# An expert stage's Silu and gate product for the next step, placed ahead of the result copies on ScalarE and VectorE

## The chip, the cores and the metric

The kernel runs on one core of one Trainium2 chip. The metric is the device time of one execution in microseconds (us); lower is better. Times are given as the median of several runs.

## What is computed

The reference is one layer of a streaming encoder: a modulated RMSNorm, an attention of two head groups, an output projection, and then a mixture of 32 experts of which each token takes two. The change is in the experts alone. What they compute, cut to the core:

```python
def expert_step(acc, args):
    wg, wu, wd, cw = args
    hh = jax.nn.silu(x @ wg) * (x @ wu)
    return acc + (hh * cw[:, None].astype(hh.dtype)) @ wd, None
```

There are 1088 tokens (1024 of the prompt and 64 of the sample), the model's width is 1024 and an expert's is 256. All is in float32.

## The kernel before, in words

The program goes through its stages one after the other: modulation and projection, attention, the output projection with the router, the experts (`experts`), and the final sum and norm (`finish`). The router writes lists that say which tokens go to which expert, in blocks of 64 rows.

The experts run in steps. A step p handles two blocks side by side, one in partitions 0 to 63 and one in 64 to 127, with the weights of two experts: those of the first half (`a_gu`, `a_dn`) stay in three slots and are loaded by SyncE when a slot is free, those of the second half (`b_gu`, three buffers, and `b_dn`, two) are loaded anew for each step by ScalarE's queue. Gate and up weights of an expert are 2 MB, the down weights 1 MB. In these runs there are 26 steps, numbered 0 to 25; the program counts them two to a round, and the rounds beyond a sure minimum stand under a branch.

What one step does, and on which engine:

- GpSimd reads the list (`listing`, L1545), gathers the 128 token rows by an indirect DMA (`gather`, L1550), and at the end scatters the 128 result rows of 4 KB to `expert_rows` in DRAM by an indirect DMA (L1572).
- TensorE transposes the rows (`transpose_x`, L1584), multiplies by gate and up (`gate_up`, L1595 and L1598, 32 matmuls into one of two PSUM banks `gu_ps`), transposes the hidden rows (`transpose_hidden`, L1605), and multiplies by the down weights (`down`, L1618 and L1621, 16 matmuls into the single `y_ps`).
- ScalarE and VectorE each move half of the transposed rows from PSUM (`move_xT`, L1671 and L1737). ScalarE computes Silu of the gate half (`silu`, L1677), VectorE multiplies by the up half (`gate_times_up`, L1741) and copies the transposed hidden rows (L1749). Both copy half of the result from `y_ps` to the single tile `y`, with the router's weight as scale: the *result copies*, L1695 on ScalarE and L1754 on VectorE.

The order is written out by hand, one body for each engine, and semaphores tie the bodies together. TensorE's body for step p is: `gate_up(p + 1)`, `transpose_hidden(p)`, `transpose_x(p + 2)`, `down(p)`. These are the waits that matter around the change:

- A result copy of step p waits for `down(p)` and for the landing of the scatter of step p - 1, since both use the one tile `y`. The scatter of step p waits for both result copies.
- `down(p + 1)` waits for the result copies of step p, since there is one `y_ps`.
- `silu(p + 1)` waits for `gate_up(p + 1)` and for `transpose_hidden(p)`, since there is one tile `gate`. `gate_times_up(p + 1)` waits for `silu(p + 1)`, and `transpose_hidden(p + 1)` for that.
- ScalarE issues the load of `b_dn` for step p + 2 behind its result copy, and the load of `b_gu` for step p + 3 at the head of its body. SyncE's load of an `a` slot (L1503 and L1505 on SPq) waits for a `down` (`y_ready`).

Of the kernel before, what the change touches and what calls it, by code (L numbers as in the profile page):

```python
# [1441 lines left out]
def experts(nc, s, a, k):  # L1442
# [33 lines left out]
    def look(eng, first, n, low, high):  # L1476
        return eng.value_load(table[0:1, first + n:first + n + 1], min_val=low, max_val=high)
# [13 lines left out]
    def following(eng, p, n, do):  # L1491

        if p // 2 < SURE:
            do()
        elif p < STEPS:
            with eng.If(n > p // 2):
                do()
            with eng.Else():
                eng.nop()

    def weights(eng, ex, gu, dn, gu_sem, dn_sem):
        if gu is not None:
            eng.dma_start(gu, a["w_gu"][bass.ds(ex, 1)].rearrange("a p k n -> p (a k) n")).then_inc(gu_sem, 16)  # L1503
        if dn is not None:
            eng.dma_start(dn, a["w_dn"][bass.ds(ex, 1)].rearrange("a p k n -> p (a k) n")).then_inc(dn_sem, 16)  # L1505

    @block.sync
    def _(sp):
        def load(m):
            r = m % SLOTS  # L1510
            ex = look(sp, T_HELD, m, 0, NE - 1) if m else look(sp, T_FIRST, 0, 0, NE - 1)
            weights(sp, ex, a_gu[:, r, :, :], a_dn[:, r, :, :], slot_ld[r], slot_ld[r])

        def landed(m):
            sp.wait_ge(slot_ld[m % SLOTS], 32 * (m // SLOTS + 1))
            sp.sem_inc(loaded, 1)

        def where(m, body):
            with sp.If(loads > m):
                body(m)  # L1520
            with sp.Else():
                sp.nop()

        def follow(m):
            last = look(sp, T_FREE, m - SLOTS, 1, STEPS)
            alone(sp, y_ready, last, waited)
            load(m)

        load(0)
        sp.wait_ge(table_set, 1)  # L1530
        loads = look(sp, T_LOADS, 0, 1, NE)
        landed(0)
        sp.wait_ge(gu_ld[1], 16)
        where(1, load)
        sp.wait_ge(dn_ld[1], 16)
        where(2, load)
        for m in range(NE - 1):
            where(m + 1, landed)
            if m + SLOTS < NE:
                where(m + SLOTS, follow)  # L1540
# [117 lines left out]
    @block.scalar  # L1658
    def _(act):
        def expert(p):  # L1660
            return look(act, T_EXPERT, p, 0, NE - 1)

        def load_gu(p, ex):
            weights(act, ex, b_gu[p % 3][:, :, :], None, gu_ld[p % 3], None)

        def load_dn(p, ex):
            weights(act, ex, None, b_dn[p % 2][:, :, :], None, dn_ld[p % 2])

        def move_xT(p):
            act.wait_ge(xT_ready, p + 1)  # L1670
            act.activation(xT[:, 0:4, :], xT_ps[:, 0:4, :], ACT.Copy).then_inc(xT_out_act, 1)  # L1671

        def silu(p):
            act.wait_ge(gu_ready, p + 1)
            if p:
                act.wait_ge(hT_ready, p)
            act.activation(gate[:, :], gu_ps[p % 2][:, 0:DE], ACT.Silu).then_inc(gate_done, 1)  # L1677

        held = [expert(p) for p in range(3)]
        for p in range(2):  # L1680
            load_gu(p, held[p])
            load_dn(p, held[p])
        move_xT(0)
        n = look(act, T_ROUNDS, 0, 1, ROUNDS)
        following(act, 2, n, lambda: load_gu(2, held[2]))
        silu(0)
        move_xT(1)

        def body(p, n):
            following(act, p + 3, n, lambda: load_gu(p + 3, expert(p + 3)))  # L1690
            following(act, p + 2, n, lambda: move_xT(p + 2))
            act.wait_ge(y_ready, p + 1)
            if p:
                act.wait_ge(scattered, 16 * p)
            act.activation(y[:, 0:512], y_ps[:, 0:512], ACT.Copy, scale=entry[:, p, 2:3].bitcast(F32))\  # L1695
               .then_inc(y_out_act, 1)
            following(act, p + 2, n, lambda: load_dn(p + 2, expert(p + 2)))
            if p % 2 == 0:
                silu(p + 1)
            else:  # L1700
                following(act, p + 1, n, lambda: silu(p + 1))

        in_rounds(act, n, body)

    @block.vector
    def _(dve):
        own = Own(dve, own_dve)
        blocks = nb[:, :, :].rearrange("p a n -> p (a n)")
        one = consts[:, K_ONES:K_ONES + 2 * NE]
        own(dve.tensor_scalar(some[:, :], blocks, 0.0, None, ALU.is_gt))  # L1710
        own(dve.tensor_tensor(first[:, :], ended[:, :], blocks, ALU.subtract), wait=False)
        own(dve.tensor_tensor_scan(rank[:, :], one, some[:, :], 0.0, ALU.mult, ALU.add))
        own(dve.scalar_tensor_tensor(first[:, :], first[:, :], steps[:, 0:1], some[:, :], ALU.is_lt, ALU.mult))
        own(dve.tensor_reduce(cols[:, 4:5], first[:, :], AX.X, ALU.add), wait=False)
        own(dve.tensor_tensor(held[:, :], done[:, 0, :], some[:, :], ALU.mult))
        own(dve.tensor_reduce(count[:, :], held[:, :], AX.X, ALU.add))
        own(dve.scalar_tensor_tensor(cols[:, 1:2], count[:, :], 1.0, cols[:, 4:5], ALU.add, ALU.min))
        own(dve.tensor_scalar(count[:, :], cols[:, 1:2], -1.0, None, ALU.add))
        own(dve.tensor_scalar(ahead_i[:, :], count[:, :], 86.0, None, ALU.mult))
        own(dve.tensor_scalar(ahead_i[:, :], ahead_i[:, :], 8, None, ALU.logical_shift_right))  # L1720
        own(dve.tensor_copy(over[:, :], ahead_i[:, :]))
        own(dve.scalar_tensor_tensor(cols[:, 0:1], over[:, :], -float(SLOTS), count[:, :], ALU.mult, ALU.add))
        own(dve.tensor_scalar(held[:, :], rank[:, :], index, None, ALU.is_le))
        own(dve.tensor_reduce(count[:, :], held[:, :], AX.X, ALU.add))
        own(dve.tensor_scalar(over[:, :], count[:, :], float(NE), -float(NE), ALU.is_ge, ALU.mult))
        own(dve.tensor_tensor(count[:, :], count[:, :], over[:, :], ALU.add))
        own(dve.tensor_scalar(cols[:, 2:3], count[:, :], float(NE - 1), None, ALU.min))
        own(dve.tensor_scalar(held[:, :], rank[:, :], -1.0, index, ALU.add, ALU.is_le))
        own(dve.tensor_tensor(held[:, :], held[:, :], blocks, ALU.mult))
        own(dve.tensor_reduce(count[:, :], held[:, :], AX.X, ALU.add))  # L1730
        dve.tensor_tensor(cols[:, 3:4], count[:, :], steps[:, :], ALU.min).then_inc(cols_done, 1)
        dve.wait_ge(table_ready, 1)
        dve.tensor_copy(table[:, T_SLOT:T_ROUNDS], y_ps[0:1, 0:4 * LOOK + 1]).then_inc(table_set, 1)

        def move_xT(p):
            dve.wait_ge(xT_ready, p + 1)
            dve.tensor_copy(xT[:, 4:8, :], xT_ps[:, 4:8, :]).then_inc(xT_out_dve, 1)  # L1737

        def gate_times_up(p):
            dve.wait_ge(gate_done, p + 1)  # L1740
            dve.tensor_tensor(gate[:, :], gate[:, :], gu_ps[p % 2][:, DE:2 * DE], ALU.mult).then_inc(hidden_done, 1)  # L1741

        move_xT(0)
        gate_times_up(0)
        move_xT(1)

        def body(p, n):
            dve.wait_ge(hT_ready, p + 1)
            dve.tensor_copy(hT[:, :, :], hT_ps[:, 0:2 * P].rearrange("p (c n) -> p c n", c=2)).then_inc(hT_out, 1)  # L1749
            following(dve, p + 2, n, lambda: move_xT(p + 2))  # L1750
            dve.wait_ge(y_ready, p + 1)
            if p:
                dve.wait_ge(scattered, 16 * p)
            dve.tensor_scalar(y[:, 512:1024], y_ps[:, 512:1024], entry[:, p, 2:3].bitcast(F32), None, ALU.mult)\  # L1754
               .then_inc(y_out_dve, 1)
            if p % 2 == 0:
                gate_times_up(p + 1)
            else:
                following(dve, p + 1, n, lambda: gate_times_up(p + 1))

        in_rounds(dve, look(dve, T_ROUNDS, 0, 1, ROUNDS), body)


# [175 lines left out]
```

## Time and profile before

| What | Value |
|---|---|
| Median of 3 runs | 1358.05 us (1355.63 to 1359.54) |
| The profiled execution's own time | 1351.79 us |
| Its span | 1349.6 us |
| TensorE busy over the span | 1161.5 us (86%) |
| VectorE, ScalarE, GpSimd busy | 518.6, 342.2, 295.1 us |
| DMA moved | 218.56 MB, mean 162 GB/s |

The page puts the program's work beside each other by engine: busy time over the whole span, then the span in 40 slices, then the queues, the chain that ended last, and the costliest groups. In the slices the experts' stage is the stretch from about 923 to 1294 us. Both TensorE and the DMA engines are busy for 8 or more tenths of most of its slices. The page's chain that ended last covers only the last few per cent of the span, so the stage has to be read from its waits and its timeline.

### The profile page before, as it was taken

The page shows a single profiled execution, that of the slowest core. Times are in us where ns is not written, and L with a number is a line of the kernel's source. Part 1 is how long each engine was busy: PE and PEld are TensorE (multiplying, and loading weights), DVE is VectorE, ACT ScalarE, POOL GpSimd, SP SyncE. Part 2 cuts the span into 40 slices and gives each one's busy share as a digit, 9 for nine tenths or more (in the row PEclk, how much of TensorE's full clock was granted, in tenths as well). Part 3 has the DMA queues.
Part 4 walks back from the last instruction along what each step waited for, and adds up shares of the span by engine and source line. Part 5 has one row for each costly group of instructions (what it writes and reads, how often), then busy time and mean ns, then how long its engine had stood idle before and what let it go on. Part 6 is the DMA issues. An engine that isn't in the chain of part 4 may idle for free. (4 is left out here: it accounts for less than half of the span.)

```text
span 1349.6 us, 19893 instructions
## 1 busy us (share of the span) xinstructions
PE 1161.5 (86%) x7175; PEld 767.0 (57%) x7175; DVE 518.6 (38%) x1320; ACT 342.2 (25%) x854; POOL 295.1 (22%) x233
## 2 busy tenths in 40 slices
PE   4688999999999999999886999951998999899846
PEld 2346888888888888888773555521333333333312
DVE  2432244444444444535533466653112121111118
ACT  4422233333332333333442222110101011111102
POOL 2031313030302121110002565533112221211001
PEclk9677999999999999999998999975999899999978
DMA  9771202020102121110130111115998999999646
GB/s 372 291 287 50 71 19 89 1 88 3 60 11 70 53 78 45 54 53 26 47 140 8 63 53 57 47 32 236 419 393 313 386 379 388 376 374 363 249 185 250
DMA packets 53538, 218.56 MB, mean 162 GB/s; under 512 B 9904, under 2 KB 26680, under 8 KB 42560
## 3 DMA queue, kind: packets, MB, share of 16 engines
q1 hardware_dynamic: 36912, 117.26, 23.7%
q10 hardware_dynamic: 7632, 82.05, 15.3%
q0 software_dynamic: 8896, 17.93, 3.4%
q8 instruction: 63, 1.03, 0.3%
q14 instruction: 35, 0.29, 0.1%
HBM read 196.62 MB, written 30.03 MB: 168 GB/s over the span
## 5 line engine op out<-in xcount | busy, mean ns | idle before, releaser
L729 PE MATMUL att_piece_ps<-hT_hi,w_hi 128*128 128x384 f32 (+1 forms) x528 | 185.2, 351 | 2.0 <-DVE att_k_lo_sb L857 0.8
L1595 PE MATMUL moe_gu_ps<-moe_a_gu_sb,moe_xT_sb 128*64 x416 | 184.4, 596 | 2.0 <-DVE moe_xT_sb L1737 2.0
L1598 PE MATMUL moe_gu_ps<-moe_b_gu_sb,moe_xT_sb 128*64 128x512 f32 x416 | 184.4, 596 | 0.0
L729 PE MATMUL att_piece_ps<-hT_hi,w_lo 128*128 128x384 f32 (+1 forms) x528 | 173.6, 329 | 0.0
L729 PE MATMUL att_piece_ps<-hT_lo,w_hi 128*128 128x384 f32 (+1 forms) x528 | 173.2, 328 | 0.0
L916 DVE COPY att_pT_sb<-att_pT_ps 128x512 f32<-128x512 f32 (+2 forms) x192 | 94.6, 521 | 134.0 <-PE att_pT_ps L790 133.4
L1200 PE MATMUL mix_y_ps<-mix_w_out_sb,mix_oT_sb 128*128 128x512 f32 (+1 forms) x288 | 127.2, 600 | 2.2 <-ACT mix_oT_sb L1268 2.2
L1595 PEld LDWEIGHTS moe_gu_ps<-moe_a_gu_sb,moe_xT_sb 128*64 128x64 f32 x416 | 57.2, 138 | 121.2 <-issue 121.2
L977 ACT ACTIVATE att_probs_sb<-att_probs_sb,att_nmax_sb 128x640 f32<-128x640 f32 (+5 forms) x144 | 101.2, 703 | 42.1 <-DVE att_nmax_sb L902 41.3
L902 DVE CUSTOM_DVE_ANT_0 att_probs_sb<-att_s_ps,att_bias_sb 128x640 f32<-128x640 f32 (+5 forms) x144 | 95.2, 662 | 26.8 <-PE att_s_ps L778 14.6
L729 PEld LDWEIGHTS att_piece_ps<-hT_hi,w_hi 128*128 128x128 f32 x528 | 99.8, 189 | 9.4 <-issue 4.7
L992 ACT ACTIVATE keep_rows_all_sb<-att_o_ps,att_rden_sb 128x64 f32<-128x64 f32 x144 | 37.2, 309 | 261.0 <-PE att_o_ps L811 261.0
L706 POOL CAST w_hi<-att_w_raw_sb 128x1024 fp32r<-128x1024 f32 x21 | 21.8, 1038 | 364.8 <-PE att_piece_ps L729 331.7
L1618 PE MATMUL moe_y_ps<-moe_a_dn_sb,moe_hT_sb 128*64 x208 | 99.2, 621 | 1.5 <-DVE moe_hT_sb L1749 0.7
L729 PEld LDWEIGHTS att_piece_ps<-hT_lo,w_hi 128*128 128x128 f32 x528 | 100.0, 189 | 0.0
L729 PEld LDWEIGHTS att_piece_ps<-hT_hi,w_lo 128*128 128x128 f32 x528 | 99.7, 189 | 0.0
L1621 PE MATMUL moe_y_ps<-moe_b_dn_sb,moe_hT_sb 128*64 128x512 f32 x208 | 99.2, 621 | 0.0
L1754 DVE TENSOR_SCALAR moe_y_sb<-moe_y_ps,moe_entries_sb 128x512 f32<-128x512 f32 x26 | 19.5, 751 | 204.2 <-DMA expert_rows<-moe_y_sb,moe_entries_sb 193.5
L1200 PEld LDWEIGHTS mix_y_ps<-mix_w_out_sb,mix_oT_sb 128*128 128x128 f32 (+1 forms) x288 | 52.9, 186 | 69.9 <-issue 67.0
L790 PE MATMUL att_pT_ps<-keep_consts_sb,att_probs_sb 128*128 128x128 f32 (+2 forms) x560 | 87.6, 278 | 1.8 <-ACT att_probs_sb L977 1.7
L1572 POOL DMA_INDIRECT expert_rows<-moe_y_sb,moe_entries_sb x26 | 26.2, 1010 | 254.0 <-DVE moe_y_sb L1754 254.0
L805 PE MATMUL att_o_ps<-att_pT_sb,att_v_rows_sb 128*64 128x128 f32 (+1 forms) x1088 | 74.4, 277 | 7.7 <-DVE att_pT_sb L916 6.5
(280 smaller groups left out, 1801.6 us busy)
## 6 DMA issues: line engine op xcount, KB each, us to landing
moe_b_gu_sb<-in_w_gu ACTq DMA_DIRECT2D x26, 2048.0 KB
moe_b_dn_sb<-in_w_dn ACTq DMA_DIRECT2D x26, 1024.0 KB
moe_a_gu_sb<-in_w_gu SPq DMA_DIRECT2D x10, 2048.0 KB
keep_rows_all_sb<-in_w_ada SPq DMA_DIRECT2D x8, 2048.0 KB, 12.2
att_w_raw_sb<-in_w_qkv SPq DMA_DIRECT2D x21, 512.0 KB, 3.3
moe_a_dn_sb<-in_w_dn SPq DMA_DIRECT2D x10, 1024.0 KB
in_w_ada_sb<-in_w_ada SPq DMA_DIRECT2D x4, 2048.0 KB, 11.5
in_x_sb<-in_x_prompt SPq DMA_DIRECT2D x8, 512.0 KB, 7.0
```

What stands on the lines that cost most here:

```text
L729: ins = pe.matmul(bank[:, 0:hi - lo], w[:, kind, kc, :], x[:, kc, lo:hi], start=(m == 0), stop=(m == 3 * NC - 1))
L790: ins = pe.transpose(pT_ps[e % 2][0:m, b - b0, 0:r], probs[h][0:r, b * P:b * P + m], ident[0:r, 0:r])
L805: ins = pe.matmul(o_ps[head, 0:r], v, pT[h][0:m, b, 0:r], start=(b == 0), stop=(b == len(kb) - 1))
L902: dve.tensor_tensor_reduce(probs[h][0:r, 0:wide], s_ps[h][0:r, 0:wide], bias, -SCALE, BIG, ALU.add, ALU.min, nmax[0:r, 2 * at + h:2 * at + ...
L916: ins = dve.tensor_copy(pT[h][:, b0:b1, :], pT_ps[e % 2][:, 0:b1 - b0, :])
L977: act.activation(probs[h][0:r, 0:wide], probs[h][0:r, 0:wide], ACT.Exp, bias=nmax[0:r, 2 * at + h:2 * at + h + 1], scale=-1.0, accum_out=d ...
L992: ins = act.activation(rows_all[0:r, t, first + HD * h:first + HD * h + HD], o_ps[0:r, P + HD * h:P + HD * h + HD], ACT.Copy, scale=rden[0 ...
L1200: ins = pe.matmul(y_ps[0:r, 512 * n:512 * n + 512], oT[:, c, 0:r], w_out[:, c, 512 * n:512 * n + 512], start=(c == 0), stop=(c == NC - 1))
L1595: pe.matmul(gu_ps[p % 2][LANE[0], :], xT[:, c, LANE[0]], a_gu[:, bass.ds(slot, 1), c, :].rearrange("p a n -> p (a n)"), start=(c == 0), st ...
L1598: ins = pe.matmul(gu_ps[p % 2][LANE[1], :], xT[:, c, LANE[1]], b_gu[p % 3][:, c, :], start=(c == 0), stop=(c == NC - 1))
L1618: pe.matmul(y_ps[LANE[0], half], hT[:, c, LANE[0]], a_dn[:, bass.ds(slot, 1), c, half].rearrange("p a n -> p (a n)"), start=(c == 0), stop ...
L1621: ins = pe.matmul(y_ps[LANE[1], half], hT[:, c, LANE[1]], b_dn[p % 2][:, c, half], start=(c == 0), stop=(c == 1))
```

## The change

In the body of step p, ScalarE now does `silu(p + 1)` before `move_xT(p + 2)`, where it did it as the last thing, behind the result copy of step p and the issue of the `b_dn` load. VectorE now does `gate_times_up(p + 1)` behind `move_xT(p + 2)` and before its result copy, where it did it behind the copy. TensorE's, GpSimd's and SyncE's programs are the same. No instruction is added or removed but some branches.

```diff
@@ ScalarE's body
             following(act, p + 3, n, lambda: load_gu(p + 3, expert(p + 3)))
+            if p % 2 == 0:
+                silu(p + 1)
+            else:
+                following(act, p + 1, n, lambda: silu(p + 1))
             following(act, p + 2, n, lambda: move_xT(p + 2))
             act.wait_ge(y_ready, p + 1)
...
             following(act, p + 2, n, lambda: load_dn(p + 2, expert(p + 2)))
-            if p % 2 == 0:
-                silu(p + 1)
-            else:
-                following(act, p + 1, n, lambda: silu(p + 1))
@@ VectorE's body
             following(dve, p + 2, n, lambda: move_xT(p + 2))
+            if p % 2 == 0:
+                gate_times_up(p + 1)
+            else:
+                following(dve, p + 1, n, lambda: gate_times_up(p + 1))
             dve.wait_ge(y_ready, p + 1)
...
                .then_inc(y_out_dve, 1)
-            if p % 2 == 0:
-                gate_times_up(p + 1)
-            else:
-                following(dve, p + 1, n, lambda: gate_times_up(p + 1))
```

VectorE's order in the first steps of the experts, before. L1749 copies the transposed hidden rows, L1737 the transposed tokens, L1754 is the result copy and L1741 the gate product of the next step:

```order
L1749 COPY moe_hT_sb<-moe_hT_ps 128x256
L1737 COPY moe_xT_sb<-moe_xT_ps 128x512
L1754 TENSOR_SCALAR moe_y_sb<-moe_y_ps,moe_entries_sb 128x512
L1741 TENSOR_TENSOR moe_gate_sb<-moe_gate_sb,moe_gu_ps 128x256
L1749 COPY moe_hT_sb<-moe_hT_ps 128x256
```

And with the change, where the result copy stands on line 1758:

```order
L1749 COPY moe_hT_sb<-moe_hT_ps 128x256
L1737 COPY moe_xT_sb<-moe_xT_ps 128x512
L1741 TENSOR_TENSOR moe_gate_sb<-moe_gate_sb,moe_gu_ps 128x256
L1758 TENSOR_SCALAR moe_y_sb<-moe_y_ps,moe_entries_sb 128x512
L1749 COPY moe_hT_sb<-moe_hT_ps 128x256
```

The gate product and the result copy have changed places; the two copies for TensorE stand where they stood.

ScalarE's order at the same place, before. L1671 moves the transposed tokens, L1695 is the result copy, L1505 and L1503 issue the loads of the down and of the gate and up weights, L1677 is the Silu:

```order
L1671 ACTIVATE moe_xT_sb<-moe_xT_ps 128x512
L1695 ACTIVATE moe_y_sb<-moe_y_ps,moe_entries_sb 128x512
L1477 TENSOR_LOAD route_table_sb
L1477 ISA x2
L1505 ISA
L1505 DMA moe_b_dn_sb<-in_w_dn 128x2048
L1677 ACTIVATE moe_gate_sb<-moe_gu_ps 128x256
L1477 TENSOR_LOAD route_table_sb
L1477 ISA x2
L1503 ISA
L1503 DMA moe_b_gu_sb<-in_w_gu 128x4096
```

And with the change, where the result copy stands on line 1699:

```order
L1671 ACTIVATE moe_xT_sb<-moe_xT_ps 128x512
L1699 ACTIVATE moe_y_sb<-moe_y_ps,moe_entries_sb 128x512
L1477 TENSOR_LOAD route_table_sb
L1477 ISA x2
L1505 ISA
L1505 DMA moe_b_dn_sb<-in_w_dn 128x2048
L1477 TENSOR_LOAD route_table_sb
L1477 ISA x2
L1503 ISA
L1503 DMA moe_b_gu_sb<-in_w_gu 128x4096
L1677 ACTIVATE moe_gate_sb<-moe_gu_ps 128x256
```

The load of the gate and up weights now follows that of the down weights with nothing between them, and the Silu behind it is already that of the next body.

## Rows read from the trace of the kernel before

**Rows 1.** Waits between engines in the stretch 967.99 to 1263.82 us: engine, line, awaited, total, times, longest

```profile
ACT moe_y_sb L1695 <- DMA expert_rows<-moe_y_sb,moe_entries_sb: 183.2, 21, 11.0
...
PE moe_hT_ps L1605 <- DVE moe_gate_sb L1741: 23.4, 15, 3.2
```

**Rows 2.** ScalarE's timeline, result copies of steps 0, 4, 22 and 23

```profile
967.99 0.69 ACT L1695 ACTIVATE moe_y_sb<-moe_y_ps,moe_entries_sb 128x512 f32<-128x512 f32 x1 [3.00 <-PE moe_y_ps L1621]
...
1027.99 0.69 ACT L1695 ACTIVATE moe_y_sb<-moe_y_ps,moe_entries_sb 128x512 f32<-128x512 f32 x1 [9.78 <-DMA expert_rows<-moe_y_sb,moe_entries_sb]
...
1263.82 0.69 ACT L1695 ACTIVATE moe_y_sb<-moe_y_ps,moe_entries_sb 128x512 f32<-128x512 f32 x1 [9.01 <-DMA expert_rows<-moe_y_sb,moe_entries_sb]
...
1271.24 0.69 ACT L1695 ACTIVATE moe_y_sb<-moe_y_ps,moe_entries_sb 128x512 f32<-128x512 f32 x1 [3.23 <-DMA expert_rows<-moe_y_sb,moe_entries_sb]
```

**Rows 3.** Scatters to expert_rows: time from issue to landing, of 26

```profile
DMA to landing us min/median/max: 3.2/11.4/17.9
```

**Rows 4.** Timeline of all engines from result copy 3: start, duration, instruction, [idle before]

```profile
1014.26 0.69 ACT L1695 ACTIVATE moe_y_sb<-moe_y_ps,moe_entries_sb 128x512 f32<-128x512 f32 x1 [9.30 <-DMA expert_rows<-moe_y_sb,moe_entries_sb]
...
1014.93 0.34 ACTq L1505 DMA_DIRECT2D moe_b_dn_sb<-in_w_dn  x1
1015.37 0.38 ACT L1677 ACTIVATE moe_gate_sb<-moe_gu_ps 128x256 f32<-128x256 f32 x1 [0.43 <-issue]
1015.79 0.42 DVE L1741 TENSOR_TENSOR moe_gate_sb<-moe_gate_sb,moe_gu_ps 128x256 f32<-128x256 f32 x1 [0.77 <-ACT moe_gate_sb L1677]
1015.88 1.02 POOL L1572 DMA_INDIRECT expert_rows<-moe_y_sb,moe_entries_sb  x1 [9.91 <-DVE moe_y_sb L1754]
1016.05 0.34 ACTq L1503 DMA_DIRECT2D moe_b_gu_sb<-in_w_gu  x1
1016.26 0.44 PE L1605 MATMUL moe_hT_ps<-keep_consts_sb,moe_gate_sb 128*128 128x128 f32 x2 [1.49 <-DVE moe_gate_sb L1741]
...
1017.61 0.69 DVE L1737 COPY moe_xT_sb<-moe_xT_ps 128x512 f32<-128x512 f32 x1 [0.45 <-PE moe_xT_ps L1584]
```

**Rows 5.** TensorE's timeline, first down matmuls of two steps in a row without a wait

```profile
1074.43 0.64 PE L1618 MATMUL moe_y_ps<-moe_a_dn_sb,moe_hT_sb 128*64 x1
...
1086.12 0.64 PE L1618 MATMUL moe_y_ps<-moe_a_dn_sb,moe_hT_sb 128*64 x1
```

**Rows 6.** TensorE's timeline after result copy 22

```profile
1266.06 0.44 PE L1605 MATMUL moe_hT_ps<-keep_consts_sb,moe_gate_sb 128*128 128x128 f32 x2 [1.33 <-DVE moe_gate_sb L1741]
...
1267.31 0.64 PE L1618 MATMUL moe_y_ps<-moe_a_dn_sb,moe_hT_sb 128*64 x1
```

**Rows 7.** Timeline of all engines from result copy 24 to result copy 25

```profile
1282.56 0.69 ACT L1695 ACTIVATE moe_y_sb<-moe_y_ps,moe_entries_sb 128x512 f32<-128x512 f32 x1 [9.54 <-PE moe_y_ps L1621]
1282.56 0.75 DVE L1754 TENSOR_SCALAR moe_y_sb<-moe_y_ps,moe_entries_sb 128x512 f32<-128x512 f32 x1 [3.90 <-PE moe_y_ps L1621]
...
1284.03 0.44 PE L1605 MATMUL moe_hT_ps<-keep_consts_sb,moe_gate_sb 128*128 128x128 f32 x2 [1.51 <-DVE moe_gate_sb L1741]
...
1284.50 0.42 DVE L1749 COPY moe_hT_sb<-moe_hT_ps 128x256 f32<-128x256 f32 x1 [0.53 <-PE moe_hT_ps L1605]
1285.13 0.64 PE L1618 MATMUL moe_y_ps<-moe_a_dn_sb,moe_hT_sb 128*64 x1 [0.66 <-DVE moe_hT_sb L1749]
...
1288.83 0.69 ACT L1695 ACTIVATE moe_y_sb<-moe_y_ps,moe_entries_sb 128x512 f32<-128x512 f32 x1 [5.31 <-PE moe_y_ps L1621]
```

**Rows 8.** Stretches: length, busy of PE, PEld, DVE, ACT, POOL, clock, DMA share, GB/s

```profile
967.99:1263.82 295.83, 272.15 (x1306) 103.38 (x1304) 50.34 (x88) 36.67 (x66) 62.72 (x62) 0.97 0.93 373
...
1027.99:1029.99 2.00, 0.03 (x2) 0.00 (x0) 1.17 (x2) 1.07 (x2) 0.38 (x1) 1.00 0.19 27
```

**Rows 9.** DMA queues from 1021 to 1026 us: packets, MB, share of 16 engines

```profile
q0 software_dynamic: 149, 0.36, 18.2%
```

**Rows 10.** The same from 1053 to 1058 us

```profile
q1 hardware_dynamic: 127, 1.89, 88.4%
q0 software_dynamic: 79, 0.17, 8.5%
```

## The prediction

> **What bounds the kernel now.** I read three views of the experts' stage: the waits, to see who waits for whom; the timelines, to see how a step closes on the next; and the stretches with their DMA share, to see what is left to win.
>
> In the waits the reader should see that ScalarE's result copy waited 21 times for the landing of a scatter, 183.2 us in all, while TensorE's hidden transposes waited 15 times for the gate product, 23.4 us in all [rows 1]. The second wait is the one that the change removes. The first decides whether that is worth anything. Between result copy 0 at 967.99 and result copy 22 at 1263.82 lie 295.83 us and 22 steps, so a step takes 13.45 us [rows 2]. Copy 0 waited for TensorE; 21 of the 22 that follow have a recorded wait for the previous scatter [rows 1, 2].
>
> One step shows how the loop closes [rows 4]: the copy starts at 1014.26, GpSimd's scatter is issued at 1015.88, 1.62 us later, and the next result copy starts at 1027.99 [rows 2], 12.1 us after the issue. A scatter takes 11.4 us from issue to landing in the median [rows 3]. So result copy, scatter, result copy is a closed loop of about 13.5 us, with neither Silu, nor gate product, nor TensorE in it. TensorE's own step, where nothing stops it, is 11.69 us from down matmul to down matmul (1074.43 to 1086.12) [rows 5]. That is 1.76 us less than the 13.45 us of the loop. TensorE's waits are that slack, showing where it is first felt.
>
> **The change, part by part.** *In the 22 steps.* Before, `transpose_hidden` could start only behind the copy, the Silu and the product: at 1016.26, 2.00 us behind the copy [rows 4]. Now Silu (0.38 us) and product (0.42 us) run some 10 us earlier, while both engines wait for the scatter. TensorE then goes on until `down`, which still waits for the result copies, 0.75 us long on VectorE [rows 7]. Its wait changes place, from the transposes to `down`, and `down` can start 0.75 us behind the copy's start instead of 2.00 + 1.25 [rows 6] = 3.25 us, but the next copy waits for the scatter. I put the 23.4 us at nothing: they are hidden by the scatter's flight.
>
> What the moved work could delay: on ScalarE the Silu now stands ahead of `move_xT`. It needs the hidden transposes, which start at 1016.26 and take 0.44 us, so it could be done by about 1017.1; `move_xT` starts at 1017.61 with VectorE's, when the token transposes are done [rows 4]. It fits. On VectorE the product comes behind the 0.69 us of `move_xT`, so it ends near 1018.7; the result copy behind it cannot start before the down matmuls end, which begin 1.25 us behind the hidden transposes [rows 6], at 1017.51, and took 3.7 us (1285.13 to 1288.83) where nothing else held the copy [rows 7]: not before 1021.2. In this step it came at 1027.99. Both cost nothing; were the scatter fast, 2.5 us of that cover would be left.
>
> *The DMA issues.* The load of the down weights still follows the result copy. That of the gate and up weights followed the Silu; now it follows the down load. It was issued at 1016.05, 0.78 us behind the end of the down load's issue at 1015.27; of this 0.48 us (1015.27 to 1015.75) go [rows 4]. Over 22 steps that is 10.6 us at the most. I take nothing: ahead of it in the same queue stands 1 MB of down weights, which at the stretch's 373 GB/s takes 2.8 us [rows 8], so the second load is in the queue in time before and after. The issue is earlier, the bytes are not. The lower end is below nothing: with an earlier `down`, SyncE's loads of the first half's weights come earlier too, and fall on the scatter. Seven of these 3 MB loads lie in the 22 steps. If each comes earlier by what TensorE waits in the mean of a step, 23.4 / 22 = 1.06 us, they move by 7.4 us together.
>
> What would that cost? In 5 us without such a load the scatter queue, q0, got 18.2% of the engines [rows 9]; in 5 us with one, on q1, it got 8.5% [rows 10]. So an earlier us of it takes (18.2 - 8.5) / 18.2 = 53% of the scatter's progress, 3.9 us over 7.4 us, if nothing of it comes back. Most should: a load that starts sooner is over sooner, and the scatter behind it goes at the better rate. I take nothing, and keep +3.9 and -10.6 us as the ends. The Trainium skill ("DMA: Bandwidth & Descriptors", Queues, rings and completion order) has an SDMA engine take turns between the queue rows that have work. By equal turns a second load would lower the scatter's share from a half to a third, cost 2.5 us, and make the sum 0; the rows have far smaller shares and a steeper loss, and I go by them.
>
> *At the end.* Here the loop opens, because the last loads are in and a scatter lands fast: copy 23 starts at 1271.24, 7.42 us behind copy 22 [rows 2]. Copy 24 starts at 1282.56 and copy 25 at 1288.83, and both waited for TensorE [rows 7]. So from copy 22 on TensorE's path sets the time.
> - After copy 22 the hidden transposes waited 1.33 us for the product and started at 1266.06; `down` started 1.25 us later at 1267.31 [rows 6]. Now the transposes start at 1264.73 and `down` at 1265.98, which is behind the copies' end (1263.82 + 0.75 = 1264.57). TensorE has no wait for another engine between this and copy 24. **-1.3 us**.
> - After copy 24 there were 2.57 us until the last `down` at 1285.13 [rows 7]. Silu, product and the transposes come off this path. What stays is VectorE's copy, 0.75 us, then the copy of the hidden rows, 0.42 us, with some 0.05 us between them, and 0.21 us until `down` (1284.92 to 1285.13): 1.43 us. **-1.1 us**.
>
> Sum: -2.4 us, 1351.79 to 1349.4 us for the profiled execution. That one was 6.3 us faster than the median of the runs; taken from the median the forecast is **1355.6 us**. The end behaves like this whatever the throttle does in between: the granted clock of the 22 steps was 0.97 of full speed [rows 8].
>
> **The rivals.**
> 1. *The loads really start sooner.* The DMA engines worked 0.93 of the 22 steps, so 7% or 20.7 us were not used, and in the 2 us behind copy 4 they worked 0.19 [rows 8]. If the earlier second issue lets each burst climb sooner, up to the 10.6 us show. For it: after such gaps both loads meet empty queues. Against it: the down load alone keeps the queue filled for 2.8 us. With half of it: 1358.05 - 2.4 - 5.3 = 1350.3 us.
> 2. *TensorE is the bound after all.* Then its 23.4 us go too: 1358.05 - 2.4 - 23.4 = 1332.2 us. For it: its clock and its busy time, 272.15 of 295.83 us [rows 8]. Against it: the result copies wait for scatters, not for matmuls [rows 1].
> 3. *Slower: the slot loads fall on the scatter.* The place is the scatter in flight whenever `down` frees a slot; the price is 7.4 us of shift at a rate c of us lost for each us moved. From c = 0.32 on it has eaten the 2.4 us and the kernel is slower; at 53% with nothing given back it is 1359.6 us, and at c = 1, when the scatter stands still meanwhile, 1363.1 us. I name 1361.3 us, between the two. For it: q0's 18.2% and 8.5% [rows 9, 10]. Against it: the bytes are the same and only change places.
> 4. *The change doesn't act*, if Silu were held by something else than the result copy. Its wait for the copy's end and for the issue of a load is plain in the timeline, 1.11 us behind the copy's start [rows 4], and gate and up matmuls of that step are done or all but done then. I give it no chance of its own; its time would be the old one, 1358.05 us.
>
> **How the numbers follow.** The forecast has 0.60, rival 1 has 0.22, rival 2 has 0.04, rival 3 has 0.14. A measurement of this kernel can tell 0.3%, 4.1 us, from no change. The forecast lies within that; since the runs themselves spread over 3.9 us I let 0.06 of its 0.60 fall on faster. Rival 1 and rival 2 count as faster; of rival 3, whose end at 1359.6 us is within 0.3% and whose end at 1363.1 us is not, a half each. Faster 0.06 + 0.22 + 0.04 = 0.32, same 0.54 + 0.07 = 0.61, slower 0.07. The range goes from 1348 us, which leaves out rival 2 and the better part of rival 1, to 1361.5 us, which leaves out the dearer half of rival 3.
>
> **What would show it.** TensorE's wait of the transposes for the product, 23.4 us, should be gone, with a shorter one at the first down matmul on the result copies in its place. The result copies should still wait about 183 us for scatters, and copies 0 to 22 still be some 296 us apart. From copy 22 to copy 25 there should be 22.6 us instead of 25.01. The forecast is wrong if the 22 steps come out more than 3 us away from 296 us, on either side: shorter with a DMA share over 0.93 is rival 1, shorter with result copies that wait for matmuls is rival 2, longer with a longer median flight of the scatter than 11.4 us is rival 3.

## The result and the profile after

The change made the kernel slower: 1369.45 us in the median of 8 runs (1368.36 to 1374.25), against 1360.7 us in the median of 8 runs of before. The ratio is 1.0073, with a 95% interval of 1.0053 to 1.0093. The forecast was 1355.6 us in a range of 1348 to 1361.5, so it had the wrong side and too narrow a range. Slower had a chance of 0.07. Of the runs below one, of the control with two gather buffers, took 2293.18 us in place of about 1364 us and is left out of its ratio.

The profiled execution of the changed kernel took 1372.16 us, with a span of 1370.0 us. I read it with the same views as the one before. First the waits of the 22 steps from result copy 0 to result copy 22, to be laid beside [rows 1]:

```profile
ACT moe_y_sb L1699 <- DMA expert_rows<-moe_y_sb,moe_entries_sb: 234.5, 22, 13.4
...
PE moe_y_ps L1618 <- DVE moe_hT_sb L1749: 34.0, 15, 4.9
```

The hidden transposes no longer wait for the gate product; no such row is left. TensorE's wait now stands at the first down matmul, for the copy of the hidden rows, which VectorE makes behind its result copy. It is 34.0 us, not less than the 23.4 us of before. The wait that sets the step has grown, from 183.2 us to 234.5 us. The result copies 0, 22, 23, 24 and 25 on ScalarE's timeline, to be laid beside [rows 2] and [rows 7]:

```profile
972.27 0.69 ACT L1699 ACTIVATE moe_y_sb<-moe_y_ps,moe_entries_sb 128x512 f32<-128x512 f32 x1 [2.99 <-PE moe_y_ps L1621]
...
1283.23 0.69 ACT L1699 ACTIVATE moe_y_sb<-moe_y_ps,moe_entries_sb 128x512 f32<-128x512 f32 x1 [10.07 <-DMA expert_rows<-moe_y_sb,moe_entries_sb]
...
1289.92 0.69 ACT L1699 ACTIVATE moe_y_sb<-moe_y_ps,moe_entries_sb 128x512 f32<-128x512 f32 x1 [4.24 <-PE moe_y_ps L1621]
...
1301.47 0.69 ACT L1699 ACTIVATE moe_y_sb<-moe_y_ps,moe_entries_sb 128x512 f32<-128x512 f32 x1 [3.88 <-PE moe_y_ps L1621]
...
1308.84 0.69 ACT L1699 ACTIVATE moe_y_sb<-moe_y_ps,moe_entries_sb 128x512 f32<-128x512 f32 x1 [6.68 <-DMA expert_rows<-moe_y_sb,moe_entries_sb]
```

The 22 steps took 310.96 us (972.27 to 1283.23), 15.1 us more than the 295.83 us of before. The end, copy 22 to copy 25, took 25.61 us, against 25.01. The two spans differ by 20.4 us; another 4.3 us lie before copy 0, where the program is the same in both (a second profile of the changed kernel, below, has copy 0 at 965.64). So the loss is in the 22 steps. The stretches show where, to be laid beside [rows 8]:

```profile
972.27:1283.23 310.96, 276.43 (x1318) 104.35 (x1314) 47.21 (x88) 34.55 (x67) 62.79 (x62) 0.96 0.90 354
```

The DMA engines worked 0.90 of it in the place of 0.93: 31.1 us were unused, 20.7 us before. The bytes are the same. So some 10.4 of the 15.1 us are time in which the DMA engines did nothing; the shares are rounded to 0.01, which is 3 us in each. A lower share alone proves no cause, since any delay with the same bytes lowers it.

One thing about this pair: it shows a larger difference than the medians do, 20.4 us against 8.75. The profiled execution of before lies 8.9 us below the median of the 8 runs of before (1351.79 and 1360.7 us), that of the changed kernel 2.7 us above its own. Outside the 22 steps the program took 1053.8 to 1061.2 us in the ten profiles that are compared by place below, so at the median of before the 22 steps would take some 300 to 307 us (an estimate), not 295.83.

**Where in the steps.** I took the starts of all result copies from ScalarE's timeline and the starts of SyncE's slot loads from its own, and split the 22 steps in those in which SyncE issued a slot load (7 of them) and the rest (15):

| | Slot load behind the result copy, us | Mean, us | Steps with one, mean us | The others, mean us |
|---|---|---|---|---|
| Before | 9.5 7.7 9.7 7.7 7.7 7.9 8.2 | 8.3 | 13.20 | 13.56 |
| Changed | 6.1 5.8 7.5 5.8 5.8 5.8 5.8 | 6.1 | 15.45 | 13.52 |

In this pair the whole loss is in the seven steps with a slot load: 7 times 2.25 is 15.7 us. Step 13 stands for them. Its result copies and its slot load before, from ScalarE's and SyncE's timelines:

```profile
1146.34 0.69 ACT L1695 ACTIVATE moe_y_sb<-moe_y_ps,moe_entries_sb 128x512 f32<-128x512 f32 x1 [9.00 <-DMA expert_rows<-moe_y_sb,moe_entries_sb]
...
1154.07 0.34 SPq L1503 DMA_DIRECT2D moe_a_gu_sb<-in_w_gu  x1
...
1158.49 0.69 ACT L1695 ACTIVATE moe_y_sb<-moe_y_ps,moe_entries_sb 128x512 f32<-128x512 f32 x1 [8.20 <-DMA expert_rows<-moe_y_sb,moe_entries_sb]
```

And in the changed kernel, with the start of its down matmuls from TensorE's timeline:

```profile
1155.81 0.69 ACT L1699 ACTIVATE moe_y_sb<-moe_y_ps,moe_entries_sb 128x512 f32<-128x512 f32 x1 [9.55 <-DMA expert_rows<-moe_y_sb,moe_entries_sb]
...
1157.11 0.64 PE L1618 MATMUL moe_y_ps<-moe_a_dn_sb,moe_hT_sb 128*64 x1 [0.59 <-DVE moe_hT_sb L1749]
...
1161.63 0.30 SPq L1503 DMA_DIRECT2D moe_a_gu_sb<-in_w_gu  x1
...
1170.97 0.69 ACT L1699 ACTIVATE moe_y_sb<-moe_y_ps,moe_entries_sb 128x512 f32<-128x512 f32 x1 [12.13 <-DMA expert_rows<-moe_y_sb,moe_entries_sb]
```

The down matmuls start 1.30 us behind the copy, in the place of 3.25. SyncE's load waits for their end, so it comes at 5.8 us in the place of 7.7. The step takes 15.16 us in the place of 12.15. The DMA queues of these two stretches (packets, MB, share of the 16 engines; q10 is ScalarE's loads, q1 SyncE's, q0 GpSimd's scatter and gathers), before:

```profile
q10 hardware_dynamic: 288, 3.15, 66.8%
q1 hardware_dynamic: 33, 0.54, 11.6%
q0 software_dynamic: 278, 0.45, 9.8%
```

Changed:

```profile
q10 hardware_dynamic: 288, 3.15, 54.6%
q1 hardware_dynamic: 125, 1.95, 30.4%
q0 software_dynamic: 193, 0.31, 5.4%
```

Both steps move the same 3.15 MB for ScalarE. Before, only 0.54 MB of the slot load passed before the scatter had landed. In the changed kernel it was 1.95 MB, and the scatter was that much later. The 1.41 MB more are 3.8 us at the 373 GB/s of [rows 8]; the step is 3.0 us longer.

**Where the DMA engines pause.** Not behind the copy that ends a step with a slot load: in the 5 us there they were busy 4.98 us before and 4.99 us in the changed kernel, in the mean of the seven. The pause comes behind the second copy after the load. The stretch of 5 us behind that copy for the load of step 5, before and changed:

```profile
1069.24:1074.24 5.00, 5.00 (x30) 2.17 (x26) 1.59 (x3) 1.07 (x2) 2.77 (x3) 1.00 0.82 288
1074.77:1079.77 5.00, 3.71 (x10) 1.14 (x12) 2.10 (x4) 1.56 (x3) 2.77 (x3) 0.68 0.61 229
```

The DMA share is 0.61 in the place of 0.82. Over the seven such pauses, 35 us, the engines were unused for 2.8 us before and for 9.0 us in the changed kernel.

### The profile page after: what moved, and what is told of

Its sections match the earlier page's. It is cut to its first block and busy times, and to the rows that moved or that the text cites. A ratio compares the mean times of both kernels' runs of the same rounds, so it can differ in the third digit from the quotient of the medians.

```text
span 1370.0 us, 19896 instructions
## 1 busy us (share of the span) xinstructions
PE 1168.4 (85%) x7175; PEld 770.1 (56%) x7175; DVE 516.2 (38%) x1320; ACT 340.5 (25%) x854; POOL 295.4 (22%) x233
## 5 line engine op out<-in xcount | busy, mean ns | idle before, releaser
L1618 PE MATMUL moe_y_ps<-moe_a_dn_sb,moe_hT_sb 128*64 x208 | 106.5, 660 | 37.4 <-DVE moe_hT_sb L1749 36.7
L1758 DVE TENSOR_SCALAR moe_y_sb<-moe_y_ps,moe_entries_sb 128x512 f32<-128x512 f32 x26 | 19.5, 751 | 251.8 <-DMA expert_rows<-moe_y_sb,moe_entries_sb 241.5
L977 ACT ACTIVATE att_probs_sb<-att_probs_sb,att_nmax_sb 128x640 f32<-128x640 f32 (+5 forms) x144 | 101.2, 703 | 43.3 <-DVE att_nmax_sb L902 42.6
L1621 PE MATMUL moe_y_ps<-moe_b_dn_sb,moe_hT_sb 128*64 128x512 f32 x208 | 106.5, 660 | 0.0
L902 DVE CUSTOM_DVE_ANT_0 att_probs_sb<-att_s_ps,att_bias_sb 128x640 f32<-128x640 f32 (+5 forms) x144 | 95.1, 661 | 27.1 <-PE att_s_ps L778 14.6
L1618 PEld LDWEIGHTS moe_y_ps<-moe_a_dn_sb,moe_hT_sb 128*64 128x64 f32 x208 | 29.1, 150 | 96.0 <-issue 96.0
## 6 DMA issues: line engine op xcount, KB each, us to landing
keep_rows_all_sb<-in_w_ada SPq DMA_DIRECT2D x8, 2048.0 KB, 11.8
```

The source lines that it names most:

```text
L902: dve.tensor_tensor_reduce(probs[h][0:r, 0:wide], s_ps[h][0:r, 0:wide], bias, -SCALE, BIG, ALU.add, ALU.min, nmax[0:r, 2 * at + h:2 * at + ...
L977: act.activation(probs[h][0:r, 0:wide], probs[h][0:r, 0:wide], ACT.Exp, bias=nmax[0:r, 2 * at + h:2 * at + h + 1], scale=-1.0, accum_out=d ...
L1618: pe.matmul(y_ps[LANE[0], half], hT[:, c, LANE[0]], a_dn[:, bass.ds(slot, 1), c, half].rearrange("p a n -> p (a n)"), start=(c == 0), stop ...
L1621: ins = pe.matmul(y_ps[LANE[1], half], hT[:, c, LANE[1]], b_dn[p % 2][:, c, half], start=(c == 0), stop=(c == 1))
```

## The experiments

The theory after the result, **theory A**: what counts is when in the step the slot load is issued. Early, it passes together with the scatter that the next copy waits for. Late, it fills a pause of the DMA engines behind a later copy. Silu and product matter only because they start TensorE sooner. The rivals: **theory B**, ScalarE's second load, now right behind its first, stands ahead of the scatter; **theory C**, the new order on VectorE costs by itself. All kernels below were timed in 10 or 12 runs each beside the kernel before.

**One part alone: the Silu.** The gate product stays behind VectorE's result copy.

```diff
 ScalarE's body
+            (silu(p + 1) as in the change)
 VectorE's body
             (gate_times_up(p + 1) as before)
```

> Silu moved as in the change, the gate product left behind VectorE's result copy. Theory A (the change is slower because the slot loads of SyncE start sooner behind a result copy: 5.8 us in the changed kernel, 7.7 us before, and so are drained before the next copy): the first down matmul should start about 2.5 us behind the copy's start (3.25 before, 1.3 changed), the slot loads at about 7.0 us, and of the 15 us that the 22 steps grew by a third, some 5 us, should show: ratio to before 1.003 to 1.005. Theory B (the second load of ScalarE, now issued directly behind the first, stands ahead of the scatter): the whole loss shows, ratio 1.007 or more, since that load comes as early here as in the changed kernel.

Measured: 1.0008 (0.9994 to 1.0022). The slot loads came at 6.9 to 8.4 us, 7.2 in the mean, the 22 steps took 304.3 us and the seven steps 14.28 us in the mean. ScalarE's second load came as early as in the changed kernel and the loss did not follow it. The profile lies between the two, as theory A wants it, but the ratio misses its 1.003 to 1.005 and can't be told from 1; the 22 steps of one execution, which scatter by some us, say less than the 12 runs.

**The other part alone: the order of the loads.**

```diff
 ScalarE's body
-            following(act, p + 3, n, lambda: load_gu(p + 3, expert(p + 3)))
+            if p == 0:
+                following(act, 3, n, lambda: load_gu(3, expert(3)))
...
             following(act, p + 2, n, lambda: load_dn(p + 2, expert(p + 2)))
+            following(act, p + 4, n, lambda: load_gu(p + 4, expert(p + 4)))
```

> The kernel before, with only the load of the gate and up weights issued directly behind that of the down weights; Silu and gate product stay behind the result copy, the Silu now behind both loads. Theory A: the slot loads move by nothing or a little later, so the 22 steps stay at 296 us within 3 us, ratio 0.998 to 1.002. Theory B: ratio 1.007, with the scatters' median flight up from 11.4 us to over 12 us.

Measured: 0.9977 (0.9958 to 0.9996). Theory B falls: the same order of the loads is no slower, and the median flight of a scatter stayed at 11.3 us. It was a little faster, which I had not expected. The Silu now stands behind two issues, TensorE starts its down matmuls at some 4.9 us, and the slot loads moved to 9.6 us in the mean.

**The change with the slot load held back.** SyncE waits for a semaphore that `gate_up` raises in its midst, in the place of `y_ready`. The three kernels differ in the matmul pair `c` that raises it.

```diff
 SyncE
-            alone(sp, y_ready, last, waited)
+            alone(sp, begun, last, waited)
 TensorE's gate_up
+                if c == 3 and p >= 2:
+                    ins.then_inc(begun, 1)
```

> The changed kernel, with SyncE's slot load held until the fourth of the eight pairs of matmuls of the gate_up that follows, so that it is issued at about 7.6 us behind the result copy, as before the change. Theory A: the loss goes, the 22 steps take 294 to 299 us, ratio to before 0.998 to 1.002. Theory B, and a third, theory C (the result copies or the down matmuls are late by themselves, since the copy of the hidden rows now stands behind VectorE's result copy): the loss stays, ratio 1.007.

> As the one before, held until the seventh pair, about 8.9 us behind the result copy. Theory A in its strong form (a slot load that straddles the next result copy fills the pause of the DMA engines there) wants this at least as fast as the earlier hold, ratio 0.994 to 1.000, and the DMA engines' unused time in the 22 steps under the 20 us of before. If what matters is only how much of the load is shared with the scatter in flight, the same. Theories B and C: 1.007.

> The changed kernel with the slot load held until the second of the eight pairs of the gate_up that follows, at about 7.6 us behind the result copy, where most of these loads stood before the change. Theory A: the time of before, ratio 0.998 to 1.002, between the 1.007 at 5.8 us and the 0.997 at 9.5 us. If only a load much later than before is harmless: 1.003 to 1.006.

Measured, with c = 1: 0.9992 (0.9968 to 1.0017), loads at 7.6 us in the mean. With c = 3: 0.997 (0.9948 to 0.9993), loads at 9.8 us; I had reckoned 7.6. With c = 6: 0.9996 (0.9975 to 1.0017), loads at 11.8 us and more (one fell 0.46 us behind the next copy), where I had reckoned 8.9. The seven steps with a load took 14.81, 12.77 and 13.57 us in the mean. All else is the changed kernel, so Silu, product and VectorE's order cost nothing by themselves once the load is away: theory C falls. The medians show it. The profile with c = 1 does so less: its seven steps took 14.81 us, not the 13.20 us of before's, and its 22 steps 302.76 us, within what the median of before is worth by the estimate above. The stretch of the 22 steps with c = 3:

```profile
965.87:1266.07 300.20, 273.22 (x1318) 103.61 (x1314) 46.93 (x88) 34.54 (x67) 62.72 (x62) 0.98 0.93 367
```

The DMA share is back at 0.93. The 22 steps of this one execution are not the 294 to 299 us of the expectation: step 16 alone took 17.9 us there, and I can't say why. The queues in step 13 (1142.72 to 1154.90, 12.18 us):

```profile
q10 hardware_dynamic: 289, 3.15, 65.9%
q0 software_dynamic: 326, 0.62, 13.1%
q1 hardware_dynamic: 8, 0.13, 5.3%
```

Now only 0.13 MB of the slot load pass beside the scatter. The strong form of theory A, the later the better, is not borne out: at some 12 us the ratio was 0.9996, not lower than at 9.8 us. Whether it is higher there isn't shown, since the intervals of the two overlap.

**The kernel before with the load held back**, c = 1, no part of the change:

> The kernel before, with SyncE's slot load held until the second of the eight pairs of the gate_up that follows. Theory A (what counts is where in the step the slot load is issued, not where Silu and gate product stand): in the changed kernel a load at 9.5 us behind the result copy gave 0.997 of the time before, at 5.8 us 1.007, at 11.8 us 0.9996. Here it should be issued at about 9.4 us, and the ratio be 0.995 to 0.999. Rival (the hold helped only because Silu and product come early): 1.000 to 1.004.

Measured: 0.9965 (0.9942 to 0.9988), loads at 9.8 us in the mean, seven steps of 12.68 us. The same place gives the same gain with Silu and product late. The stretch:

```profile
969.61:1263.88 294.27, 268.53 (x1296) 102.63 (x1294) 50.33 (x88) 36.68 (x66) 62.70 (x62) 0.98 0.94 374
```

**The kernel before with an early load.** This puts the suspected cause in alone. SyncE may load the gate and up part of a slot during the down matmuls, since these don't read it.

```diff
 SyncE
+            alone(sp, begun, last, waited)
             weights(sp, ex, a_gu[:, r, :, :], None, slot_ld[r], None)
+            alone(sp, y_ready, last, waited)
             weights(sp, ex, None, a_dn[:, r, :, :], None, slot_ld[r])
 TensorE's down
+                    if n == 0 and c == 1:
+                        first.then_inc(begun, 1)
```

> The kernel before, Silu and gate product where they were, but SyncE issues the 2 MB gate and up part of a slot load when half of the down matmuls are done, at about 6.1 us behind the result copy in the place of 7.7; the 1 MB down part follows as soon as the down matmuls are over. Theory A (where the slot load falls in the step is the whole cause): slower, ratio 1.003 to 1.008, the seven steps with such a load at 14.5 to 15.5 us in the mean (13.2 before, 15.45 changed), the others unchanged at 13.5. Rival (the early Silu and product, and the copy of the hidden rows behind VectorE's result copy, have a share of their own): 0.998 to 1.002.

> The changed kernel once more, on the chip of the two runs above, to have them beside it. Ratio 1.005 to 1.009, 22 steps of 308 to 314 us, steps with a slot load above 15 us in the mean and the others at 13.5 us.

Measured on the same chip: the early load alone 1.0045 (1.0021 to 1.007), the changed kernel again 1.0069 (1.0045 to 1.0092). The early loads came at 6.0 to 7.6 us, 6.5 in the mean; the seven steps took 15.10 us and the others 13.50. The changed kernel had 15.45 and 13.38 us this time, and 308.86 us for the 22 steps. Waits and stretch of the early load:

```profile
ACT moe_y_sb L1701 <- DMA expert_rows<-moe_y_sb,moe_entries_sb: 202.6, 22, 11.9
...
PE moe_hT_ps L1609 <- DVE moe_gate_sb L1747: 31.3, 14, 4.2
```

```profile
967.02:1275.23 308.21, 276.70 (x1299) 105.21 (x1297) 50.32 (x88) 36.69 (x67) 62.71 (x62) 0.95 0.90 358
```

TensorE's wait for the product is still there, and the DMA share is 0.90 all the same. The loss came without the change. It is 1.0045 at 6.5 us and 1.0069 at 5.9 us; the intervals overlap, so a small share of the change's own is neither shown nor excluded. The pauses behind the second copy after a load agree: over the seven, the DMA engines were unused for 9.0 us (changed), 7.7 (changed, again), 9.1 (early load), 6.1 (Silu alone) and 5.2 us (held c = 1), but for 2.8 us at most in before and in all four kernels with loads at 9.6 us or later. By place, all ten kernels with one tile `y` and three gather buffers:

| Mean place of the slot load, us | Kernel | Ratio |
|---|---|---|
| 5.9 | changed, again | 1.0069 |
| 6.1 | changed | 1.0073 |
| 6.5 | before, early load | 1.0045 |
| 7.2 | Silu alone | 1.0008 |
| 7.6 | changed, held c = 1 | 0.9992 |
| 8.3 | before | 1 |
| 9.6 | before, loads in the new order | 0.9977 |
| 9.8 | changed, held c = 3 | 0.997 |
| 9.8 | before, held c = 1 | 0.9965 |
| about 12 | changed, held c = 6 | 0.9996 |

**Opening the loop.** Two tiles `y`, so that a copy waits for the scatter before the last. The second tile is the third gather buffer, so that no more SBUF is needed. The kernel after it is the control for that.

```diff
-    y = s.sb("y", [P, D])
+    y = [s.sb("y", [P, D]), x[2]]
...
-            if p:
-                act.wait_ge(scattered, 16 * p)
+            if p >= 2:
+                act.wait_ge(scattered[p % 2], 16 * (p // 2))
```

> The kernel before with two tiles y, so that a result copy waits for the scatter before the last; the second tile is the third gather buffer, so gathers run one step less ahead. If the loop of copy, scatter and copy sets the step: the 183 us of waits for scatters go, and the 22 steps fall from 296 us to what is next, the DMA engines' 276 us of work or TensorE's 257 us; ratio 0.980 to 0.990. If it does not set it: 0.997 to 1.003.

> The changed kernel with the same two tiles y. If the change only costs by way of the scatter in flight, then with that loop open the loss is gone: within 0.3% of e6_before_two_y. If the early slot load costs in any order of the rest: 0.5% or more behind e6_before_two_y.

> A control for the two above: the kernel before with two gather buffers in the place of three, and one tile y. A gather is issued a step later and still some 10 us before its transposes, so ratio 0.998 to 1.003; if TensorE waits for gathers, more.

Measured: before with two tiles 1.0081 (1.0051 to 1.011), changed with two tiles 1.0047 (1.0022 to 1.0072), control 1.0022 (0.9998 to 1.0045). Without the loop the changed kernel is no longer the slower of the two: it is 0.5% below the other, which misses the 0.3% named, and their intervals overlap. The pair does not test the place, though: in both the slot loads come 0.8 us behind a copy, so the change no longer moved them. In the control they came at 0.4 to 0.8 us four times and at 9.3 to 11.8 us three times. My expectation for the level missed too, and the profile of before with two tiles says why. Waits in its stretch 968.23 to 1265 us:

```profile
ACT route_x_sb L1696 <- PE moe_y_ps L1622: 34.9, 11, 4.9
...
PE moe_xT_ps L1585 <- DMA route_x_sb<-h_rows,moe_entries_sb: 27.2, 7, 4.8
```

No wait for a scatter is left: the loop is open. TensorE now waits 7 times for a gather. On ScalarE's timeline, a step without a slot load, the step with one (issued at 1053.28), and the step behind it:

```profile
1040.81 0.69 ACT L1696 ACTIVATE route_x_sb<-moe_y_ps,moe_entries_sb 128x512 f32<-128x512 f32 x1 [2.99 <-PE moe_y_ps L1622]
1052.50 0.69 ACT L1696 ACTIVATE moe_y_sb<-moe_y_ps,moe_entries_sb 128x512 f32<-128x512 f32 x1 [3.00 <-PE moe_y_ps L1622]
1064.19 0.69 ACT L1696 ACTIVATE route_x_sb<-moe_y_ps,moe_entries_sb 128x512 f32<-128x512 f32 x1 [2.99 <-PE moe_y_ps L1622]
1083.71 0.69 ACT L1696 ACTIVATE moe_y_sb<-moe_y_ps,moe_entries_sb 128x512 f32<-128x512 f32 x1 [4.98 <-PE moe_y_ps L1622]
```

Copies 11.69 us apart twice, exactly TensorE's own step of [rows 5]; then one 19.52 us after the last. In all seven cases the step with the slot load took 11.69 or 11.70 us and the step behind it 17.6 to 19.5 us. TensorE's timeline in this one:

```profile
1076.13 1.97 PE L1585 MATMUL moe_xT_ps<-keep_consts_sb,route_x_sb 128*128 128x128 f32 x8 [4.75 <-DMA route_x_sb<-h_rows,moe_entries_sb]
```

A gather was late by 4.75 us, and the transposes behind it took 1.97 us. So the 22 steps took 311.34 us with the loop open, no less than with it: as soon as the scatter no longer sets the step, the gathers do, and the DMA engines are busy for 0.89 of the time.

**All together**: changed, two tiles, load held at c = 6.

> The changed kernel with two tiles y, two gather buffers, and the slot load held until the seventh pair of the gate_up that follows. With two tiles y alone (e7_changed_two_y) steps without a slot load ran at TensorE's 11.69 us, and 7 times TensorE waited some 4 us for a gather that a slot load held up. If the slot load's place is what holds the gather up, the later place (about 7 us behind the result copy in the place of 0.8) ends these waits: 22 steps of 265 to 280 us, ratio to before 0.975 to 0.990. If the DMA engines are simply full, or the later load is itself missed by TensorE: 0.995 to 1.005.

Measured: 1.0024 (1.0002 to 1.0046), the load at 6.8 us behind the copy before it. TensorE still waited 8 times for gathers, 28.2 us in the stretch 965 to 1300 us:

```profile
PE moe_xT_ps L1586 <- DMA route_x_sb<-h_rows,moe_entries_sb: 28.2, 8, 4.4
```

Seven of the eight waits stood in the steps behind those with a slot load; the steps with one took 11.69 us, as with two tiles alone, and it is the step behind that the expectation should have named. So the later slot load did not bring the gathers in time. Whether a third gather buffer would wasn't tried. The three kernels whose whole interval lies below before's time are those with one tile and the load at 9.6 to 9.8 us, with or without the change.

## Why the prediction was wrong

**What bounds the kernel** held for the step: it is the loop of result copy, scatter and result copy. Opening it brought steps of 11.69 us, but no shorter time in all; the DMA engines, busy for some 275 of the 295.83 us, leave little below the loop. Nothing that only TensorE gained came out as time. The 23.4 us were worth nothing, as said.

**Silu, product and `move_xT`** held: changed with the load at 7.6 us is as fast as before (0.9992).

**ScalarE's second load** at nothing held, and so rival 1 fell (0.9977 with the order alone, which the moved slot loads account for in the table).

**SyncE's loads are the step that failed**, "Most should: a load that starts sooner is over sooner ... I take nothing". Two errors are in it. *The size of the shift.* I took it from TensorE's mean wait, 1.06 us a load and 7.4 us together. But what frees a slot is the end of `down`, and the text itself had its start going from 3.25 to about 0.75 us behind the copy. The seven places add up to 58.4 us before and to 42.6 us with the change: the loads moved by 15.8 us together, 2.3 us each. The copy of the hidden rows, in VectorE's order behind the result copy, kept `down` at 1.30 us. *The rate.* I expected up to 53% with most of it given back, and so took nothing. The 22 steps of the profiled pair grew by 15.1 us, 0.96 us for each us of shift; those of the second profile by 13.0 us over 17.3 us of shift, 0.75; the medians differ by 8.75 us, 0.55 for each us. The rate is open between these. In none of them was most of it given back: the steps without a slot load stayed at 13.52 us (13.56 before), and the bytes that had filled the pause behind the second copy were gone by then. With the measured 15.8 us of shift, the 53% of the prediction with nothing given back is 8.4 us, close to the medians' 8.75. That the two agree is in part luck: the rows behind the 53% compare the scatter beside ScalarE's loads alone with the scatter beside SyncE's load almost alone (q10 had 1.6% in the second window), not a second load added to the first, and another window of before without a slot load (1178 to 1183 us) has 14.6% for q0 in the place of 18.2%, which would make it 42%.

Two smaller parts of the miss: the forecast started from the median of 3 runs, 1358.05 us, where 8 runs gave 1360.7, and it counted 2.4 us of gain at the end (below). Rival 3 had the mechanism, and its rates from 0.53 to 1 hold what was measured; but on 7.4 us of shift its dearest time was 1363.1 us, 6.4 us below the result. It got 0.14 because I called the bytes conserved. They are, but a closed loop loses time, not bytes.

**The rule of the Trainium skill** ("DMA: Bandwidth & Descriptors", Queues, rings and completion order), that the engines take turns between the queues with work, was taken as equal shares, and gave an estimate of 2.5 us on the 7.4 us of shift. On the 15.8 us that were measured it would be 5.3 us, below the medians' 8.75. In step 13 q0 got 9.8% of the engines before and 5.4% after, 45% less; that lies between the third of equal shares and the 53% of the rows, and since q0 carries gathers too, it decides nothing.

**The end** was to give 2.4 us and gave nothing in the profiled pair: 25.61 us, not 22.6. After copy 22, `down` started at 1.29 us in the place of 3.49, so 2.2 us earlier and not 1.3. But its matmuls took 1.5 us longer, since the clock had fallen behind TensorE's wait of 1.76 us (start and duration on TensorE's timeline):

```profile
1285.17 1.06 PE L1618 MATMUL moe_y_ps<-moe_a_dn_sb,moe_hT_sb 128*64 x1
...
1286.02 1.06 PE L1618 MATMUL moe_y_ps<-moe_a_dn_sb,moe_hT_sb 128*64 x1
...
1288.41 0.59 PE L1618 MATMUL moe_y_ps<-moe_a_dn_sb,moe_hT_sb 128*64 x1
...
1288.84 0.59 PE L1618 MATMUL moe_y_ps<-moe_a_dn_sb,moe_hT_sb 128*64 x1
```

The stretch of these matmuls, and the one behind it (the granted clock is the third number from the end):

```profile
1284.52:1288.40 3.88, 3.88 (x10) 1.22 (x12) 0.82 (x2) 0.87 (x2) 0.99 (x1) 0.56 0.82 291
1288.40:1292.00 3.60, 3.60 (x20) 1.34 (x18) 0.75 (x1) 0.69 (x1) 0.49 (x1) 1.00 0.25 67
```

The matmuls follow each other at 0.85 us and then again at 0.43 us, the levels of 1.2 and 2.4 GHz; the prediction said that the end would behave the same whatever the throttle does. The last `down` did come at 1.28 us behind copy 24, near the 1.43 us reckoned, but copy 25 then waited 6.68 us for a scatter, where before it had waited for TensorE. I had not put the scatter next in line. In the second profile of the changed kernel the clock stayed at 1.00 over this end and copy 24 came 2.2 us sooner behind copy 22 than in before's, but copy 25 waited 6.99 us for a scatter again, and the end took 24.22 us. So the scatter is the part that repeats, and the end gave 0.8 us at best.

**Rival 2** fell, since TensorE's wait only moved. **What would make it wrong** named the right sign, 22 steps over 3 us from 296; but the sign that I gave for rival 3, a median flight over 11.4 us, hardly shows it (11.6 us), since only seven of the flights are longer.

That the place of the slot load is the cause is shown in both directions: put in alone it makes the kernel before slower, taken out it makes the changed kernel as fast as before. How the loss divides between the two ways, a scatter that lands later and a pause that stays empty, no run separates. Why nothing more is gained past 10 us is open.

## What to carry to other kernels

When a change lets an engine finish sooner in a loop that something else bounds, list what its finish releases, and read from the timeline how far each release moves; a free gain of slack is a change of the DMA schedule. A prefetch that nobody is in a hurry for need not start as early as its buffer allows: try it later, away from a small transfer that a loop waits for. Here nearly 4 us of delay were worth 1% of the kernel (1.0073 to 0.997), with one semaphore. And read steps by kind: means over all steps and the median flight hid what the seven steps with a slot load showed at once. Look at more than one execution before a size is taken from it; this pair showed 20.4 us where the medians differ by 8.75.

## What the hardware showed that I had not expected

- A small DMA from GpSimd's queue is very late beside large loads: 11.4 us from issue to landing in the median [rows 3], and 3.3 and 3.2 us for the last two, with almost nothing else in the queues (1284 to 1294 us). With only the place of the 3 MB loads changed, the steps with one went from 12.8 us (changed, held c = 3) to 15.5 us (changed) in the mean.
- A wait of 4.75 us cost TensorE more than itself: the eight transposes behind it took 1.97 us at a granted clock of 0.50 (the level of 1.2 GHz), against 1.04 us in step 13 of the changed kernel, where TensorE had not paused; and in the changed kernel's last steps down matmuls behind a pause of 1.76 us came at half rate. It is not so behind each pause: in the second profile of the changed kernel the same matmuls ran at 1.00, and in before with two tiles the transposes behind a wait of 3.98 us took 1.09 us. Where the bound is TensorE, such a wait has to be counted with what follows it.
